# Second branch's scores: fp32 products over 64 rows, or two fp32r products over 128 rows

## The chip, the cores and the metric

The kernel runs on one core of one Trainium2 chip. The time is the device time of one execution in microseconds; the median of several runs is given. TensorE multiplies, VectorE (DVE), ScalarE (ACT) and GpSimd (POOL) do elementwise work, and SyncE (SP) issues nearly all transfers.

## The reference, cut to what matters

One layer of a decoder for 512 tokens of width 1024, all in float32. A token mixer with three attention branches is followed by a gated merge, an output projection and a SwiGLU. The change touches only the scores of the second branch, differential attention with 4 heads of 2 x 64 query and key columns:

```
logits = einsum('bqhmd,bshmd->bmhqs', q, k) * ATTN_SCALE + bias     # m = 0, 1; d = 64
p = softmax(where(dist >= 0, logits, -inf))
attn = p[:, 0] - lam * p[:, 1];   out = einsum('bhqs,bshe->bqhe', attn, v)
```

## The kernel before, in words

Large products are not made in plain fp32. Each operand is split into a rounded part (hi, type fp32r, a copy on ScalarE) and the rest (lo, a subtraction on VectorE), and TensorE adds three fp32r products, hi*hi, hi*lo and lo*hi (lines 862 to 864 and 1216 to 1218). The index scores of the first branch (lines 1025 and 1027) need two products: the query's hi part stands in 64 partitions and its lo part in the other 64, the key's hi part is doubled, and one product of 128 rows gives (hi+lo)*hi.

The attention is one loop over steps v = 0 to 87, written out in the same order on every engine (lines 1224, 1599, 2050). Steps 0 to 31 are the third branch, 32 to 63 the first (8 heads, 4 query blocks each), 64 to 79 the second (4 heads, 4 query blocks), and the rest are dense work. In the second branch a step is query block i = v % 4 of head h = (v - 64) // 4; it sees 128 * (i + 1) keys and has two score products, m = 0 and m = 1. Their operands lie in `bqk`, m = 0 in partitions 0 to 63 and m = 1 in 64 to 127; both are fp32 (line 1113), and each leaves two records in the trace.

In a step v from 66 on TensorE does, in order: the scores of v; 9 or 6 dense fp32r products of 512 columns for a tile `z` (none in steps 75 and 79); the transposes of the probabilities of v - 2; the products with the values of v - 3 (line 1160; line 1157 in the first branch). Scores go to two banks `s_ps`, one for each m, so a score product waits until VectorE has read the one two before it (`shifted`). Dense tiles have two banks `tile_ps`, freed by ScalarE (line 1442) or by VectorE's split (line 2038). VectorE, for step v: adds the bias to scores m = 0 (`shift`, line 2029), takes reciprocals, shifts m = 1, mixes the two probabilities of v - 1 (line 2069) after GpSimd has scaled one of them (line 798), makes the lo part of a weight chunk (line 1821, in steps 68 and 76 here), and splits tiles. ScalarE: exponentials (line 1580), copies of tiles, hi parts (1435), copies of transposed probabilities (1592).

Every engine works through its list in order. SyncE's list has 12 bias tables `tab` (line 642), each waiting for `shifted`, with four weight loads between them.

Of the kernel before, what the change touches and what calls it, by code (L numbers as in the profile page):

```python
# [66 lines left out]
OC_STEPS = (51, 57)  # L67
Z_STEPS = (66, 69, 72, 76, 80, 84)
# [155 lines left out]
def hybrid_block(nc, a, out):  # L224
# [10 lines left out]
    with ctx:  # L235
# [50 lines left out]
        ob_hi = place("ob_hi", R + 49, [P, 4, S], F32R)  # L286
        ob_lo = place("ob_lo", R + 57, [P, 4, S], F32R)
# [11 lines left out]
        w_uv = place("w_uv_sb", R + 121.25, [P, A_H, DH])  # L299

# [10 lines left out]
        e_raw = place("e_raw", R + 49, [P, 4, HW])  # L311
        e_lo = place("e_lo", R + 49, [P, 4, HW], F32R)
        e_hi = place("e_hi", R + 57, [P, 4, HW], F32R)
# [6 lines left out]
        mg_hi = place("mg_hi", R + 69, [P, KT, S], F32R)  # L320
# [105 lines left out]
        c_exp_made = sem("c_exp_made")  # L426
        lam_exped = sem("lam_exped")
# [30 lines left out]
        masked = sem("masked")  # L458
        recip_made = sem("recip_made")
# [13 lines left out]
        c_exped = sem("c_exped")  # L473
# [87 lines left out]
        def _(sp):  # L561
# [65 lines left out]
            load(20, [(KT, 0, cols(COL_Z, CW))])  # L627
            for n in range(A_H + B_H):
# [209 lines left out]
        def _(pe):  # L838
# [251 lines left out]
            def scores(k):  # L1090
# [20 lines left out]
                else:  # L1111
                    h, m = (v - MIX_B) // 4, k % 2
                    mm = pe.matmul(ps[:, 0:w], bqk[DH * m:DH * m + DH, h, i * P:(i + 1) * P],
                                   bqk[DH * m:DH * m + DH, 4 + h, 0:w], start=True, stop=True)
# [308 lines left out]
        def _(act):  # L1423
# [22 lines left out]
            act.activation(c_exp, c_col, ACT.Exp, scale=-1.0).then_inc(c_exp_made, 1)  # L1446
# [44 lines left out]
            act.activation(lam_e, lam_s, ACT.Exp).then_inc(lam_exped, 1)  # L1491
# [106 lines left out]

            for v in range(N_STEP):
# [22 lines left out]
                if v == 42:  # L1622
                    act.wait_ge(c_dif_made, 1)
                    act.activation(c_exp2, c_dif, ACT.Exp).then_inc(c_exped, 1)
# [180 lines left out]
        def _(dve):  # L1805
# [23 lines left out]
            dve.wait_ge(c_exp_made, 1)  # L1829
# [78 lines left out]
            dve.wait_ge(lam_exped, 1)  # L1908
# [139 lines left out]

            n_split = 0
# [369 lines left out]
```

## Time and profile before

| | us |
|---|---|
| median of 3 runs | 1000.14 |
| lowest and highest run | 998.85 and 1000.86 |
| span of the profiled execution | 997.8 |
| TensorE busy in the span | 982.7 (98%) |

The profiled execution is given by its span, from the first to the last instruction; the time around the span is not part of the page. The lowest and highest run are 1.05 and 3.06 us above that span. Busy time of TensorE is modelled: a matmul's record reaches beyond the start of the next one, so costs are best read from start to start.

### The profile page before, as it was taken

How to read it: one execution, taken by the hardware profiler on the slowest of the kernel's cores; microseconds unless marked ns; L12 is line 12 of the kernel's file. 1: busy time of each engine (PE TensorE's matmuls, PEld its weight loads, DVE VectorE, ACT ScalarE, POOL GpSimd, SP SyncE). 2: the span in 40 equal slices, each digit the busy share in tenths (PEclk: the TensorE clock that was granted, in tenths of full speed). 3: DMA queues.
4: the chain of work that ended last, by engine and by line, in shares of the span. 5: the costliest groups of instructions: out<-in, count | busy, mean ns of one | idle time of the engine just before them, and what ended most of it. 6: DMA issues, size and time to landing. Idle time of an engine off the chain costs nothing.

```text
span 997.8 us, 12705 instructions
## 1 busy us (share of the span) xinstructions
PE 982.7 (98%) x4925; PEld 804.8 (81%) x4925; DVE 481.4 (48%) x827; ACT 379.0 (38%) x679; POOL 103.2 (10%) x137
## 2 busy tenths in 40 slices
PE   7999999999999999999999999999999999999997
PEld 4778888878878767788888888988888888888886
DVE  3764778832245445664655563634433433331324
ACT  5355332254566657542223233533223222221322
POOL 1500000000065612100000002000000000000401
PEclk9999999999999999999999999999999999999999
DMA  8742836212131201265556642123444334232312
GB/s 329 230 126 85 282 119 184 90 43 85 64 108 33 64 23 33 74 207 169 191 170 211 232 139 84 64 84 105 119 150 146 111 105 148 84 106 85 127 43 85
DMA packets 88163, 123.13 MB, mean 123 GB/s; under 512 B 4824, under 2 KB 69941, under 8 KB 87986
## 3 DMA queue, kind: packets, MB, share of 16 engines
q1 hardware_dynamic: 87442, 115.98, 35.6%
q0 software_dynamic: 528, 6.22, 2.1%
q8 instruction: 32, 0.52, 0.2%
q10 hardware_dynamic: 144, 0.26, 0.1%
q14 instruction: 17, 0.14, 0.0%
HBM read 119.77 MB, written 8.45 MB: 128 GB/s over the span
## 4 chain that ended last, share of the span: by engine, by line
PE 94%; issue 2%; POOL 1%; DMA 1%; ACT 1%; DVE 0%; SPq 0%; POOLq 0%; DVEq 0%
PE tile_ps L862 18%; PE tile_ps L864 18%; PE tile_ps L863 18%; PE t_ps L1128 2%; PE o_ps L1157 2%; PE s_ps L1110 2%; PE tile_ps L1309 1%; PE s_ps L1309 1%; PE t_ps L1309 1%; PE tile_ps L1311 1%; PE s_ps L1311 1%; PE t_ps L1311 1%; PE tile_ps L1310 1%; PE s_ps L1310 1%; PE t_ps L1310 1%
## 5 line engine op out<-in xcount | busy, mean ns | idle before, releaser
L862 PE MATMUL tile_ps<-h_hi,w_hi 128*128 128x512 f32 x736 | 291.0, 395 | 0.2 <-ACT z L1442 0.2
L863 PE MATMUL tile_ps<-h_lo,w_hi 128*128 128x512 f32 x736 | 286.8, 390 | 0.0
L864 PE MATMUL tile_ps<-h_hi,w_lo 128*128 128x512 f32 x736 | 286.7, 390 | 0.0
L1821 DVE TENSOR_TENSOR w_lo<-w_raw,w_hi 128x2048 fp32r<-128x2048 f32 (+3 forms) x60 | 130.7, 2179 | 154.2 <-ACT w_hi L1435 153.5
L862 PEld LDWEIGHTS tile_ps<-h_hi,w_hi 128*128 128x128 f32 x736 | 138.1, 188 | 36.2 <-issue 6.6
L864 PEld LDWEIGHTS tile_ps<-h_hi,w_lo 128*128 128x128 f32 x736 | 138.1, 188 | 29.2
L863 PEld LDWEIGHTS tile_ps<-h_lo,w_hi 128*128 128x128 f32 x736 | 138.2, 188 | 27.6 <-issue 0.2
L1435 ACT ACTIVATE w_hi<-w_raw 128x2048 fp32r<-128x2048 f32 (+3 forms) x60 | 107.3, 1788 | 39.9 <-DMA w_raw<-in_w_branch_c_dram 9.2
L1818 DVE TENSOR_TENSOR t_lo<-t_raw,t_hi 128x2048 fp32r<-128x2048 f32 (+1 forms) x15 | 32.8, 2184 | 85.6 <-ACT t_hi L1433 85.5
L1433 ACT ACTIVATE t_hi<-t_raw 128x2048 fp32r<-128x2048 f32 (+1 forms) x15 | 27.0, 1799 | 81.5 <-PE s_ps L1311 53.5
L1580 ACT ACTIVATE nl<-nl,cst 128x256 f32<-128x256 f32 (+3 forms) x81 | 42.8, 530 | 33.0 <-DVE cst L2029 32.7
L1768 ACT ACTIVATE f_hi<-f_t 128x512 f32 (+1 forms) x22 | 13.9, 633 | 88.3 <-DVE f_t L2326 88.3
L784 POOL TENSOR_TENSOR tm<-tab,score 128x256 f32<-128x256 f32 (+2 forms) x24 | 26.6, 1107 | 177.2 <-DVE cst L2029 177.2
L1762 ACT ACTIVATE silu_t<-tile_ps 128x512 f32<-128x512 f32 x22 | 13.1, 599 | 72.0 <-PE tile_ps L864 71.9
L2326 DVE TENSOR_TENSOR f_t<-tile_ps,silu_t 128x512 f32<-128x512 f32 x20 | 13.8, 692 | 54.7 <-PE tile_ps L864 54.7
L1592 ACT ACTIVATE pt<-t_ps 128x128 f32<-128x128 f32 (+2 forms) x80 | 29.6, 408 | 21.4 <-PE t_ps L1128 20.3
L819 POOL TENSOR_TENSOR x<-gated,x 128x512 f32<-128x512 f32 x4 | 5.1, 1295 | 297.2 <-DVE gated L2247 297.2
L2165 DVE SCALAR_TENSOR_TENSOR ada_sum<-ada,cst,ada_sum 128x1024 f32<-128x1024 f32 x21 | 26.9, 1283 | 0.7
L1975 DVE MAX8 cst<-score 128x8 f32<-128x256 f32 (+2 forms) x48 | 25.1, 552 | 1.4
L1983 DVE MATCH_REPLACE8 score<-cst,score 128x256 f32<-128x256 f32 (+2 forms) x48 | 25.8, 543 | 0.0
L1128 PE MATMUL t_ps<-ident,nl 128*128 128x128 f32 x160 | 24.4, 274 | 0.0
L807 POOL TENSOR_TENSOR x<-gated,x_res 128x512 f32<-128x512 f32 x4 | 5.1, 1291 | 184.4 <-DVE gated L2247 184.4
(404 smaller groups left out, 1680.8 us busy)
## 6 DMA issues: line engine op xcount, KB each, us to landing
w_raw<-in_w_in_dram SPq DMA_DIRECT2D x31, 1024.0 KB, 5.6
w_raw<-in_w_gate_up_dram SPq DMA_DIRECT2D x22, 1024.0 KB, 6.9
ada<-in_w_ada_dram SPq DMA_DIRECT2D x12, 1024.0 KB, 5.5
t_raw<-in_w_down_dram SPq DMA_DIRECT2D x10, 1024.0 KB, 5.0
row_copies<-row_flat POOLq DMA_DIRECT2D x1, 5632.0 KB, 20.9
ada<-in_w_ada_dram SPq DMA_DIRECT2D x8, 640.0 KB, 12.0
ada<-in_w_ada_dram SPq DMA_DIRECT2D x8, 512.0 KB, 4.2
ada<-in_w_ada_dram SPq DMA_DIRECT2D x8, 384.0 KB, 9.6
```

The source lines that it names most:

```text
L862: pe.matmul(dst[0:mw, :], wh, x_hi[:, kx, :], start=start, stop=False)
L863: pe.matmul(dst[0:mw, :], wh, x_lo[:, kx, :], start=False, stop=False)
L864: mm = pe.matmul(dst[0:mw, :], wl, x_hi[:, kx, :], start=False, stop=stop)
L1128: mm = pe.transpose(t_ps[v % 2][:, j * P:(j + 1) * P], src[:, j * P:(j + 1) * P], ident[:])
L1309: pe.matmul(bank[:], x_hi[:, kx, blk], wh[:, kw, :], start=start, stop=False)
L1310: pe.matmul(bank[:], x_hi[:, kx, blk], wl[:, kw, :], start=False, stop=False)
L1311: mm = pe.matmul(bank[:], x_lo[:, kx, blk], wh[:, kw, :], start=False, stop=stop)
L1435: hi = nc.scalar.activation(w_hi[s][:, 0:kt, 0:n_cols], w_raw[s][:, 0:kt, 0:n_cols], ACT.Copy)
L1580: act.activation(b, b, ACT.Exp, bias=negmax[:, k:k + 1], scale=-1.0, accum_out=expsum[:, k:k + 1]).then_inc(exped, 1)
L1592: act.activation(pt[v % 2][:, 0:w], t_ps[v % 2][:, 0:w], ACT.Copy).then_inc(pt_ready, 1)
L1818: dve.tensor_tensor(t_lo[s][:, 0:wide, :], t_raw[s][:, 0:wide, :], t_hi[s][:, 0:wide, :].bitcast(F32), ALU.subtract).then_inc(w_split[s], 1)
L1821: dve.tensor_tensor(w_lo[s][:, 0:kt, 0:n_cols], w_raw[s][:, 0:kt, 0:n_cols], w_hi[s][:, 0:kt, 0:n_cols].bitcast(F32), ALU.subtract) \
```

## The change

The operands of the second branch's scores are stacked. For head h and m there are three new tiles of 128 x 512 in fp32r: `bq_st` (query hi in its own 64 partitions, query lo in the other 64), `bk_st` (key hi in both halves) and `bl_st` (key lo in its own half, zeros in the other). A score is then the sum of two fp32r products of 128 rows. Sixteen hi copies on ScalarE (one at the end of each of steps 42 to 45, 58 to 61, 66 to 69 and 70 to 73), sixteen subtractions on VectorE one step later, six of them behind a memset to zero, and eight transfers of 64 partitions x 2 KB within the SBUF, issued by SyncE behind the 5th, 9th, 11th and 12th bias table, prepare them. TensorE waits for them ahead of each head's first score. There are three sets of tiles; head 3 uses head 0's again. To make room, `ob_hi` and `ob_lo`, `e_raw`, `e_lo` and `e_hi` move to R + 69 and R + 77, and `mg_hi` moves to R + 49. Three one-off semaphores for small exponentials become one (`small_exped`), waited for at 1, 2 and 3; this is left out below.

```diff
 OC_STEPS = (51, 57)
+STACK_STEPS, TWICE_AFTER = (42, 58, 66, 70), (4, 8, 10, 11)
 Z_STEPS = (66, 69, 72, 76, 80, 84)
...
     return (v - 73) // 4 if 73 <= v <= 85 and (v - 73) % 4 == 0 else None
+def stack_hi_at(v):
+    for h, v0 in enumerate(STACK_STEPS):
+        if v0 <= v < v0 + 4:
+            return h, v - v0
+    return None
+def stack_of(h):
+    return h % 3
...
         oa_lo = place("oa_lo", R + 41, [P, 4, S], F32R)
-        ob_hi = place("ob_hi", R + 49, [P, 4, S], F32R)
-        ob_lo = place("ob_lo", R + 57, [P, 4, S], F32R)
+        ob_hi = place("ob_hi", R + 69, [P, 4, S], F32R)
+        ob_lo = place("ob_lo", R + 77, [P, 4, S], F32R)
         oc_hi = place("oc_hi", R + 93, [P, 2, S], F32R)
...
         w_uv = place("w_uv_sb", R + 121.25, [P, A_H, DH])
+        b_at = ((49, 51, 53, 55, 57, 59), (61, 63, 65, 67, 103, 105), (12, 14, 25, 107.25, 119.25, 121.25))
+        bq_st, bk_st, bl_st = ([[place(f"{n}{j}_{m}", R + b_at[j][2 * o + m], [P, S], F32R) for m in range(2)]
+                                for j in range(3)] for o, n in enumerate(("bq_st", "bk_st", "bl_st")))
...
             load(20, [(KT, 0, cols(COL_Z, CW))])
+            def key_twice(h):
+                j = stack_of(h)
+                for m in range(2):
+                    d0, d1 = DH * m, DH - DH * m
+                    sp.wait_ge(b_hi_made, 4 * h + m + 1)
+                    sp.dma_start(bk_st[j][m][d1:d1 + DH, :].bitcast(F32), bk_st[j][m][d0:d0 + DH, :].bitcast(F32)) \
+                        .then_inc(bk_twice[h % 2], 16)
             for n in range(A_H + B_H):
...
                 sp.dma_start(tab[n % 2][:], toeplitz(FL_AB + n * W_AB, W_AB, 1, S)).then_inc(tab_in[n % 2], 16)
+                if n in TWICE_AFTER:
+                    key_twice(TWICE_AFTER.index(n))
                 if n == 2:
...
                     h, m = (v - MIX_B) // 4, k % 2
-                    mm = pe.matmul(ps[:, 0:w], bqk[DH * m:DH * m + DH, h, i * P:(i + 1) * P],
-                                   bqk[DH * m:DH * m + DH, 4 + h, 0:w], start=True, stop=True)
+                    j = stack_of(h)
+                    if i == 0 and m == 0:
+                        pe.wait_ge(b_lo_made, 4 * h + 4)
+                        pe.wait_ge(bk_twice[h % 2], 32 * (h // 2) + 32)
+                    q_b = bq_st[j][m][:, i * P:(i + 1) * P]
+                    pe.matmul(ps[:, 0:w], q_b, bk_st[j][m][:, 0:w], start=True, stop=False)
+                    mm = pe.matmul(ps[:, 0:w], q_b, bl_st[j][m][:, 0:w], start=False, stop=True)
                 mm.then_inc(scores_made, 1)
...
+            def stack_hi(h, n):
+                j, m = stack_of(h), n % 2
+                if n == 0 and h < 2:
+                    act.wait_ge(o_made[1], MIX_A // 8)
+                elif n == 0 and h == 2:
+                    act.wait_ge(masked, 3 * A_H)
+                    wait_tile_made(act, ATT_TILE["qlat", A_H - 1])
+                elif n == 0:
+                    act.wait_ge(scores_made, MIX_B + 8)
+                rows = slice(DH * m, DH * m + DH)
+                act.activation((bq_st if n >= 2 else bk_st)[j][m][rows, :], bqk[rows, 4 - 4 * (n // 2) + h, :], ACT.Copy) \
+                    .then_inc(b_hi_made, 1)
             for v in range(N_STEP):
...
                         evacuate(ATT_TILE["qlat", h], qlat[h % 3][:, :])
+                if stack_hi_at(v) is not None:
+                    stack_hi(*stack_hi_at(v))
                 if ob_at(v) is not None:
...
                     dve.reciprocal(recip[:, u:u + 1], expsum[:, u:u + 1]).then_inc(recip_made, 1)
+            def stack_lo(h, n):
+                j, m = stack_of(h), n % 2
+                d0, d1 = DH * m, DH - DH * m
+                own, other = slice(d0, d0 + DH), slice(d1, d1 + DH)
+                dve.wait_ge(b_hi_made, 4 * h + n + 1)
+                if n >= 2:
+                    dve.tensor_tensor(bq_st[j][m][other, :], bqk[own, h, :], bq_st[j][m][own, :].bitcast(F32),
+                                      ALU.subtract).then_inc(b_lo_made, 1)
+                    return
+                if h < 3:
+                    if h == 1:
+                        wait_tile_made(dve, ATT_TILE["oc", 1])
+                    elif h == 2:
+                        wait_tile_made(dve, ATT_TILE["uv", A_H - 1])
+                    dve.memset(bl_st[j][m][other, :].bitcast(F32), 0.0)
+                dve.tensor_tensor(bl_st[j][m][own, :], bqk[own, 4 + h, :], bk_st[j][m][own, :].bitcast(F32),
+                                  ALU.subtract).then_inc(b_lo_made, 1)
...
                         .then_inc(oc_mixed, 1)
+                if v and stack_hi_at(v - 1) is not None:
+                    stack_lo(*stack_hi_at(v - 1))
                 h = (v - 71) // 4
```

## Rows read from the trace of the kernel before

**Rows 1.** The page, busy time: engine, microseconds, share of the span, instructions.
```profile
PE 982.7 (98%) x4925; PEld 804.8 (81%) x4925; DVE 481.4 (48%) x827; ACT 379.0 (38%) x679; POOL 103.2 (10%) x137
```

**Rows 2.** Windows: length, busy time of each engine, clock, share of DMA.
```profile
300.00:310.00 10.00, 10.00 (x64) 7.33 (x63) 5.58 (x20) 6.18 (x18) 5.17 (x7) 1.00 0.10 27
...
367.90:382.20 14.30, 14.13 (x79) 10.29 (x78) 8.64 (x26) 8.42 (x30) 2.44 (x4) 1.00 0.13 38
```

**Rows 3.** Timeline of TensorE, steps 71 to 73: start, length, engine, line.
```profile
379.09 1.13 PE L1113 MATMUL s_ps<-bqk 64*128 64x512 f32 x4
380.15 0.50 PE L862 MATMUL tile_ps<-h_hi,w_hi 128*128 128x512 f32 x1
380.49 0.40 PE L863 MATMUL tile_ps<-h_lo,w_hi 128*128 128x512 f32 x1
...
382.18 0.49 PE L1113 MATMUL s_ps<-bqk 64*128 64x128 f32 x4
382.60 0.50 PE L862 MATMUL tile_ps<-h_hi,w_hi 128*128 128x512 f32 x1
...
385.66 0.70 PE L1113 MATMUL s_ps<-bqk 64*128 64x256 f32 x4
386.29 0.50 PE L862 MATMUL tile_ps<-h_hi,w_hi 128*128 128x512 f32 x1
```

**Rows 4.** Line 1113's weight loads in step 69: ns min/median/max, first and last start.
```profile
L1113 PEld LDWEIGHTS s_ps<-bqk x4: 183/184/186, 370.7 to 370.8; 64*128 64x128 f32 x4
```

**Rows 5.** Chain of waits, three index score products of 256, 384, 512 columns.
```profile
75.78 0.12 PE s_ps L1025
...
77.41 0.17 PE s_ps L1025
...
79.15 0.23 PE t_ps L1025
```

**Rows 6.** Timelines of TensorE: eight loads of line 1160, one product of line 1177.
```profile
378.00 0.97 PEld L1160 LDWEIGHTS o_ps<-bv,pt 128*128 128x128 f32 x8
...
366.32 1.07 PE L1177 MATMUL tile_ps<-olat,w_uv_sb 128*64 128x512 f32 x2
```

**Rows 7.** Timelines of VectorE, then TensorE, round steps 68 to 70.
```profile
369.11 0.68 DVE L2038 TENSOR_TENSOR oa_lo<-tile_ps,oa_hi 64x512 fp32r<-64x512 f32 x1 [2.78 <-ACT oa_hi L1597]
369.83 0.29 DVE L2029 CUSTOM_DVE_ANT_0 nlb<-s_ps,tab 128x128 f32<-128x128 f32 x1
...
371.78 2.28 DVE L1821 TENSOR_TENSOR w_lo<-w_raw,w_hi 128x2048 fp32r<-128x2048 f32 x1
373.98 0.42 DVE L2029 CUSTOM_DVE_ANT_0 nl<-s_ps,tab 128x256 f32<-128x256 f32 x1
...
371.58 0.50 PE L862 MATMUL tile_ps<-h_hi,w_hi 128*128 128x512 f32 x1 [0.17 <-ACT z L1442]
...
374.96 0.92 PE L1113 MATMUL s_ps<-bqk 64*128 64x384 f32 x4
```

**Rows 8.** Timelines of TensorE, then VectorE, steps 75 and 76.
```profile
393.55 1.13 PE L1113 MATMUL s_ps<-bqk 64*128 64x512 f32 x4
...
396.13 0.49 PE L1113 MATMUL s_ps<-bqk 64*128 64x128 f32 x2 [0.19 <-DVE cst L2029]
...
394.71 0.69 DVE L2029 CUSTOM_DVE_ANT_0 nlb<-s_ps,tab 128x512 f32<-128x512 f32 x1 [1.28 <-PE s_ps L1113]
```

**Rows 9.** A group by line: shapes, count, busy us, mean ns, idle before.
```profile
L1679 ACT ACTIVATE mg_hi<-mg 128x512 fp32r<-128x512 f32 x8 | 4.9, 633 | 33.7 <-DVE mg L2191 33.7
```

**Rows 10.** Timelines of GpSimd, one form at two places, then VectorE beside the second.
```profile
277.11 0.37 POOL L793 TENSOR_SCALAR nl<-nl,cst 128x128 f32<-128x128 f32 x1
...
286.04 2.41 POOL L793 TENSOR_SCALAR nl<-nl,cst 128x128 f32<-128x128 f32 x1
...
285.74 2.47 DVE L1821 TENSOR_TENSOR w_lo<-w_raw,w_hi 128x2048 fp32r<-128x2048 f32 x1
```

**Rows 11.** DMA issues: count, size, median microseconds to landing.
```profile
tab<-row_copies SPq DMA_DIRECT2D x12, 256.0 KB, 2.7
```

More of the change, by code:

```diff
@@ L310, in hybrid_block @@
         t_lo = [place(f"t_lo{b}", 64 + 8 * b, [P, 4, HW], F32R) for b in range(2)]
-        e_raw = place("e_raw", R + 49, [P, 4, HW])
-        e_lo = place("e_lo", R + 49, [P, 4, HW], F32R)
-        e_hi = place("e_hi", R + 57, [P, 4, HW], F32R)
+        e_raw = place("e_raw", R + 69, [P, 4, HW])
+        e_lo = place("e_lo", R + 69, [P, 4, HW], F32R)
+        e_hi = place("e_hi", R + 77, [P, 4, HW], F32R)
         sig_a = place("sig_a", R + 17, [P, 2, S])
@@ L319, in hybrid_block @@
         ada2 = [place(f"ada2_{b}", R + 105 + 8 * b, [P, 2, D]) for b in range(2)]
-        mg_hi = place("mg_hi", R + 69, [P, KT, S], F32R)
+        mg_hi = place("mg_hi", R + 49, [P, KT, S], F32R)
         x_res = place("x_res", R + 33, [P, NBLK, D])
@@ L425, in hybrid_block @@
         kv_sq = sem("kv_sq")
-        c_exp_made = sem("c_exp_made")
-        lam_exped = sem("lam_exped")
+        small_exped = sem("small_exped")
         dn_used = sem("dn_used")
@@ L458, in hybrid_block @@
         masked = sem("masked")
+        b_hi_made = sem("b_hi_made")
+        b_lo_made = sem("b_lo_made")
+        bk_twice = [sem("bk_twice0"), sem("bk_twice1")]
         recip_made = sem("recip_made")
@@ L472, in hybrid_block @@
         c_dif_made = sem("c_dif_made")
-        c_exped = sem("c_exped")
         oc_mixed = sem("oc_mixed")
@@ L1445, in _ @@
             act.wait_ge(cols_ready, 1)
-            act.activation(c_exp, c_col, ACT.Exp, scale=-1.0).then_inc(c_exp_made, 1)
+            act.activation(c_exp, c_col, ACT.Exp, scale=-1.0).then_inc(small_exped, 1)
             for b in range(NBLK):
@@ L1490, in _ @@
             act.wait_ge(lam_dot, 1)
-            act.activation(lam_e, lam_s, ACT.Exp).then_inc(lam_exped, 1)
+            act.activation(lam_e, lam_s, ACT.Exp).then_inc(small_exped, 1)
             def query_hi(t):
@@ L1623, in _ @@
                     act.wait_ge(c_dif_made, 1)
-                    act.activation(c_exp2, c_dif, ACT.Exp).then_inc(c_exped, 1)
+                    act.activation(c_exp2, c_dif, ACT.Exp).then_inc(small_exped, 1)
                 if dense_ending_at(v) is not None and dense_ending_at(v)[0] == "z":
@@ L1828, in _ @@
             dve.tensor_copy(pcol, s_ps[0][:, 0:81]).then_inc(cols_ready, 1)
-            dve.wait_ge(c_exp_made, 1)
+            dve.wait_ge(small_exped, 1)
             link(dve.tensor_scalar(c_exp, c_exp, 1.0, None, ALU.add))
@@ L1907, in _ @@
             dve.tensor_scalar(g_sub_s, g_sub, 1.0 - LAM_INIT, None, ALU.mult)
-            dve.wait_ge(lam_exped, 1)
+            dve.wait_ge(small_exped, 2)
             link(dve.tensor_tensor(neg_lam, lam_e[:, 1:2], lam_e[:, 0:1], ALU.subtract))
@@ L2104, in _ @@
                 if v == 43:
-                    dve.wait_ge(c_exped, 1)
+                    dve.wait_ge(small_exped, 3)
                     dve.tensor_tensor(c_wgt[:, 0:16], c_exp2[:, 0:16], expsum[:, 0:16], ALU.mult)
```

## The prediction

> **What bounds the kernel now.** I read the page first: TensorE is busy for 982.7 of 997.8 us [rows 1], so time on its path counts, and time on another engine counts only where TensorE waits for it. Then the windows, to see which engine could run out in the stages that are touched: the granted clock is 1.00 throughout (the 2.4 GHz level), and VectorE is busy for 5.58 of 10 us in the first branch, where head 0's tiles would be made, but for 8.64 of 14.30 us in steps 68 to 71, beside ScalarE's 8.42 [rows 2]. There VectorE is the engine to watch. Then the timelines of TensorE and VectorE over steps 67 to 76, and the chain of waits over the index scores, which already have the form that the change brings in [rows 3 to 8].
>
> **TensorE, wide steps.** A step's two score products cost, from their start to that of the next instruction, 1.06 us for 512 columns (379.09 to 380.15), 0.85 for 384 (its group of 0.92 at 374.96, less the 0.07 by which the other groups reach past the next start), 0.63 for 256 (385.66 to 386.29) and 0.42 for 128 (382.18 to 382.60) [rows 3, 7]. The new form is four fp32r products, as the index scores have them: 0.23, 0.17 and 0.12 us each for 512, 384 and 256 columns [rows 5], hence 0.92, 0.68 and 0.48 us. That saves 0.14, 0.17 and 0.15 us; each width comes four times, so 0.46 x 4 = 1.84 us.
>
> Why so little, when half of the fp32 passes seem to go? Because the two old products do not follow one another. The four weight loads of a step start within 0.1 us, 370.7 to 370.8 [rows 4], and a single fp32 product of 128 rows and 512 columns is a group of 1.07 us [rows 6], nearly as long as both products of 64 rows together, 1.13 [rows 3]. So m = 0 and m = 1 run side by side in the two halves of the array, and stacking gives that up.
>
> The Trainium skill speaks against the change here (TensorE: Matmul & The Clock Gate, "Part 3: Packing small matmuls — row/col tiling"): products over few rows, placed in different row strips, run at the same time. By that rule the trace agrees, 1.06 us for two. Had they run one behind the other, a wide step would cost about 2.0 us and the change would save about 1.1 us in each.
>
> **TensorE, steps of 128 columns.** No fp32r product of 128 columns is in the trace. From below: eight weight loads of 128 columns take 0.97 us as a group, 0.19 the last [rows 6], so one starts every (0.97 - 0.19) / 7 = 0.11 us, and four products need 0.44 us against 0.42 now. From above: if such a short fp32r product were served like fp32, it would cost two of these slots, 0.22 us, and the step 0.88. I take 0.44, since 256 columns cost just 0.12 [rows 5] and half of that lies under the load's pace: four steps lose 0.08 us, and at the other end 1.84 us.
>
> **TensorE, change of type.** After fp32 work the first fp32r product delays its successor: 380.15 to 380.49 is 0.34 us where 0.23 is usual [rows 3, 5]. That 0.11 us now stands behind the scores, and will stand in front of them: no difference, except in steps 65, 75 and 79, which have no dense fp32r work and gain a change: 3 x 0.11 = 0.33 us lost. TensorE's own sum is 1.84 - 0.08 - 0.33 = 1.43 us saved.
>
> **Latency of the first score.** In a step of 512 columns VectorE starts on m = 0 at 394.71, 1.16 us after the scores began at 393.55 [rows 8]; the pair ends together. In the new order m = 0 takes 0.46 us, and with the 0.10 us between the pair's end and VectorE's start (1.16 - 1.06) and the 0.11 of the change of type it would be 0.67 us: VectorE starts 0.5 us earlier. This counts where a chain through VectorE holds TensorE. One place is step 76: its second score starts at 396.13 after a wait, because VectorE is still at step 75's scores [rows 8]. I book 0.5 us there, in place of step 75's own saving.
>
> **The preparation.** A hi copy of 64 x 512: the nearest row is a copy of 128 x 512 within the SBUF, 0.63 us on ScalarE [rows 9]; a subtraction of 64 x 512: 0.68 us on VectorE, at 369.11; records there overlap by 0.08 (371.78 + 2.28 against the next start at 373.98) [rows 7], so 0.6 us of the queue. A memset of 64 x 512 has no row: between nothing and the 0.68 of a subtraction. I take 0.4, since it reads nothing. So a subtraction behind a memset is 1.0 us. All in all VectorE gains 16 x 0.6 + 6 x 0.4 = 12 us of work, ScalarE 16 x 0.63 = 10. On ScalarE each copy ends a step's list, ahead of exponentials that wait for VectorE: I take it as hidden, bounds 0 and 0.6 us in step 68.
>
> For heads 0 and 1 I cost it at nothing: their work falls in steps 42 to 46 and 58 to 62 of the first branch, where VectorE is idle over 4 us in 10 [rows 2] and the scores run four steps ahead of their use. If that cover is thin, what is late is the reciprocal, with it GpSimd's scaling and the transposes; bounds 0 and 1 us. For head 3 too: steps 71 to 74, after the tight spot, bounds 0 and 0.6. The transfers land in about 2.7 us, as a table of 256 KB does [rows 11], and each is due steps later; on SyncE they wait for hi copies of an earlier step, so the weight load of chunk 23 queued behind them loses next to nothing, bounds 0 and 0.3. The moved tiles and the merged semaphore cost nothing: no order or wait changes with them.
>
> Head 2 is not free. Its first subtraction (with memset) stands in step 67 between VectorE's split at 369.11 and its shift at 369.83 [rows 7]. That shift is on TensorE's path: shift, exponentials, then ScalarE frees the bank of tile z, and the dense product at 371.58 has waited for exactly that [rows 7]. Against the 1.0 us stand the 0.5 us of latency in step 67, from which this chain starts, and the 0.19 us that TensorE had saved up to there (steps 64 to 66: -0.02 + 0.04 + 0.17): net the dense product is 0.31 us late. The second subtraction (again with memset) comes behind the weight chunk's lo part at 371.78 and ahead of the shift at 373.98: that shift is 0.31 + 1.0 late, done at 374.40 (its 0.42 us) + 1.31 = 375.71. The scores of step 70 (374.96 [rows 7]) need its bank: 0.75 us late, of which 0.17 comes back in that step. So TensorE enters step 71 0.58 us late, and all savings up to there are used up.
>
> **Sum.** Steps 71 to 79: 0.14 - 0.02 + 0.15 + 0.17 (steps 71 to 74), 0.5 (75 and the wait in 76), -0.02 (76), 0.15 + 0.17 + 0.03 (77 to 79) = 1.27 us. 1.27 - 0.58 = 0.69 us faster, so the span goes from 997.8 to about 997.1. The median stands 2.3 us above that span; what lies around it is unchanged, so 1000.14 - 0.69 = 999.4 us.
>
> **Rivals.** *All preparation is hidden.* For it: VectorE waits 1.28 us for TensorE before 394.71 and TensorE's wait at 371.58 is 0.17 us only [rows 7, 8]. Against it: the place of head 2's subtractions. The time: 1.43 + 0.5 - 0.03 (step 75's own share) = 1.9 us saved, 998.2.
>
> *The short steps lose.* One mechanism, in steps 64, 68, 72 and 76: fp32r of 128 columns at fp32's pace, 0.88 us in place of 0.42. That is 1.84 - 0.08 = 1.76 us on top: -0.69 + 1.76 = 1.1 us slower than before, 1001.2. It decides from 0.61 us a step on (0.69 / 4 + 0.44). For it only that no row shows such a product; against it the smooth 0.23, 0.17, 0.12 [rows 5].
>
> *VectorE's queue bites fully.* If the latency gain does not come, because the shifts are bound by VectorE's own work anyhow, steps 69 and 70 lose 0.5 us more and step 76 gives 0.5 less: -0.69 + 1.0 = 0.3 us slower, 1000.4. GpSimd could add to it: a scaling of 128 columns takes 0.37 us at one place and 2.41 at another, from 286.04 to 288.45, where VectorE was in a subtraction of two SBUF operands until 288.21 [rows 10]; the sixteen new ones are of that kind, and each could hold GpSimd for 0.6 us, with the mixing behind it. I put that at up to 1 us in steps 44 to 48, where a scaling comes right before its transposes: 1001.4 at worst.
>
> The Trainium skill has this as a rule (SBUF — State Buffer, the parts on the shared port pair): a VectorE instruction with two SBUF inputs and a GpSimd instruction that reads the SBUF exclude one another for the whole instruction. The trace agrees with it at 2.41 us.
>
> **Chances.** The forecast 0.48, with 998.8 to 1000.3 as its own range; all hidden 0.20; the short steps 0.14; VectorE's queue 0.18. What a measurement of this kernel can tell from no change is about 0.2%, 2 us. All hidden comes just short of it, and with luck in other waits passes it: faster by more than 0.2% 0.19. The short steps together with some of the queue would pass it upward: slower 0.13. Within 0.2%: 0.68. The range takes in the hidden case with its spread and the queue at its worst: 997.6 to 1001.8.
>
> **What would show it.** Four records of 0.23 us a wide step and groups of about 0.92 us show the saving; a first shift 0.67 us after the scores' start shows the latency. The price of 128 columns can be read in step 72 directly. A subtraction of 0.6 to 0.7 us and a memset right before the shifts of steps 68 and 69, and waits of TensorE for ScalarE's copy of z and for the shift ahead of step 70, show the loss; no such waits speak for the hidden case. Waits in steps 44 to 49 would show GpSimd held. The prediction is wrong in kind if the scores take more than 1.06 us at 512 columns, or if the stage from step 64 to 80 changes by more than 2 us either way.

## The result: slower by 0.33%, where no change was forecast

The changed kernel takes 1003.46 us (median of 7 runs, 1002.55 to 1004.03) where the kernel before takes 1000.67 us (7 runs). The ratio of the runs is 1.0033, with a 95% interval of 1.0023 to 1.0043 (the two medians alone give 1.0028). The forecast was 999.4 with a range up to 1001.8, so both time and range are missed. The profiled execution has a span of 1002.0 us against 997.8; these two lie further apart, by 4.2 us, than the ratio says (3.3), so the traces are read for where time goes, and the runs for how much it is in all.

The page's line of busy time, after, answers to [rows 1]:

```profile
PE 982.5 (98%) x4925; PEld 809.5 (81%) x4925; DVE 495.8 (49%) x849; ACT 386.7 (39%) x695; POOL 104.5 (10%) x137
```

TensorE is busy for as long as before, and the span is 4.2 us longer: TensorE waits more. VectorE has 14.4 us of new work and ScalarE 7.7. Two windows answer to those of [rows 2], the second again from the start of step 68 to that of step 72:

```profile
300.00:310.00 10.00, 9.65 (x60) 6.92 (x59) 6.50 (x21) 7.75 (x20) 3.64 (x6) 1.00 0.21 53
369.24:384.77 15.53, 13.65 (x79) 11.33 (x78) 12.40 (x32) 10.08 (x34) 2.45 (x4) 1.00 0.16 45
```

TensorE had 10.00 of 10 us in the first and now has 9.65. In the second VectorE is busy for 12.40 of 15.53 us (8.64 of 14.30 before), and TensorE, idle for 0.17 before, is idle for 1.88. The clock is 1.00 in both.

**Where the time went, step by step.** For each step I took the start of its scores in two traces and subtracted. The change of this difference from one row to the next is what the stage between them gained or lost; a constant part says nothing. (In e2 only head 0 is prepared, in e1 the products are the old ones; both are described below.)

```
start of the scores, us later than in the kernel before
step      after     e1       e2
42        +0.22   -0.86    +1.46
54, 62    +2.39   +1.30    +1.74     head 0's preparation lies between
68        +1.33   +1.30    +0.66
71        +2.95   +3.65    +0.04     head 2's
74        +2.02   +3.62    -0.89
77        +3.52   +4.98    -2.02     head 3's
79        +3.11   +4.99    -2.43
```

The changed kernel loses 2.17 us between steps 42 and 54, 0.72 net between 62 and 79, 0.8 right behind step 79 (the values' group of eight products, at 416.96 before, starts at 420.85, 3.89 late) and 0.3 in the 575 us behind that, which I did not follow. With the 0.22 at the start, which lies ahead of all of the change's work, this is the 4.2 us.

**The products themselves gain more than forecast.** Timeline of TensorE in the changed kernel, steps 71 and 72, which answers to [rows 3]:

```profile
382.04 0.48 PE L1146 MATMUL s_ps<-bk_st,bq_st 128*128 128x512 f32 x1
382.35 0.40 PE L1147 MATMUL s_ps<-bl_st,bq_st 128*128 128x512 f32 x1
382.58 0.39 PE L1146 MATMUL s_ps<-bk_st,bq_st 128*128 128x512 f32 x1
...
383.04 0.39 PE L890 MATMUL tile_ps<-h_hi,w_hi 128*128 128x512 f32 x1
...
384.77 0.31 PE L1146 MATMUL s_ps<-bk_st,bq_st 128*128 128x128 f32 x1
...
385.14 0.28 PE L1147 MATMUL s_ps<-bl_st,bq_st 128*128 128x128 f32 x1
385.25 0.45 PE L890 MATMUL tile_ps<-h_hi,w_hi 128*128 128x512 f32 x1
```

Read starts, not lengths: 382.04 to 383.04 is 1.00 us for 512 columns (before 1.06), 384.77 to 385.25 is 0.48 for 128 (before 0.42). An fp32r product of 128 columns starts every 0.11 to 0.12 us: the rival of the short steps is out. And yet e2's column falls by 0.36 us in a step of 512 columns (from 0.04 at step 71 to -0.32 at step 72), not by 0.06. The rest lies around the scores; section e4 has it.

**Head 2.** VectorE, then TensorE, in the changed kernel round steps 68 to 70, which answers to [rows 7]:

```profile
370.37 0.68 DVE L2087 TENSOR_TENSOR oa_lo<-tile_ps,oa_hi 64x512 fp32r<-64x512 f32 x1 [2.78 <-ACT oa_hi L1630]
371.11 0.48 DVE L2113 MEMSET bl_st<- 64x512 f32 x1
371.61 0.68 DVE L2114 TENSOR_TENSOR bl_st<-bqk,bk_st 64x512 fp32r<-64x512 f32 x1
372.22 0.28 DVE L2078 CUSTOM_DVE_ANT_0 nlb<-s_ps,tab 128x128 f32<-128x128 f32 x1
...
374.16 2.28 DVE L1870 TENSOR_TENSOR w_lo<-w_raw,w_hi 128x2048 fp32r<-128x2048 f32 x1
...
376.99 0.69 DVE L2114 TENSOR_TENSOR bl_st<-bqk,bk_st 64x512 fp32r<-64x512 f32 x1
377.71 0.42 DVE L2078 CUSTOM_DVE_ANT_0 nl<-s_ps,tab 128x256 f32<-128x256 f32 x1
```

```profile
372.56 0.39 PE L1146 MATMUL s_ps<-bk_st,bq_st 128*128 128x256 f32 x1 [0.46 <-DVE cst L2078]
...
373.95 0.50 PE L890 MATMUL tile_ps<-h_hi,w_hi 128*128 128x512 f32 x1 [0.62 <-ACT z L1475]
...
378.20 0.45 PE L1146 MATMUL s_ps<-bk_st,bq_st 128*128 128x384 f32 x1 [0.80 <-DVE cst L2078]
```

The chain is the one forecast: memset and subtraction before the shift (a second memset stands at 376.49), then the copy of z late (0.62, where e2, with nothing prepared for head 2, waits 0.26), then the scores of step 70 (0.80). It has one link more, the scores of step 69 (0.46).

**Head 3.** Three engines of the changed kernel, ahead of step 75 (ScalarE, VectorE, TensorE), which answer to [rows 8]:

```profile
393.99 0.63 ACT L1643 ACTIVATE bq_st<-bqk 64x512 fp32r<-64x512 f32 x1
394.65 0.69 ACT L1630 ACTIVATE ob_hi<-tile_ps,cst 128x512 fp32r<-128x512 f32 x1
```

```profile
388.37 0.69 DVE L2114 TENSOR_TENSOR bl_st<-bqk,bk_st 64x512 fp32r<-64x512 f32 x1
...
390.14 0.41 DVE L2078 CUSTOM_DVE_ANT_0 nl<-s_ps,tab 128x256 f32<-128x256 f32 x1
...
395.37 0.75 DVE L2089 SCALAR_TENSOR_TENSOR ob_lo<-tile_ps,cst,ob_hi 128x512 fp32r<-128x512 f32 x1 [3.08 <-ACT ob_hi L1630]
396.04 0.55 DVE L2078 CUSTOM_DVE_ANT_0 nl<-s_ps,tab 128x384 f32<-128x384 f32 x1
```

```profile
396.65 0.50 PE L1146 MATMUL s_ps<-bk_st,bq_st 128*128 128x512 f32 x1 [1.18 <-DVE cst L2078]
...
398.63 0.49 PE L1193 MATMUL o_ps<-bv,pt 128*128 128x128 f32 x2 [0.29 <-ACT pt L1625]
400.03 0.33 PE L1146 MATMUL s_ps<-bk_st,bq_st 128*128 128x128 f32 x1 [0.24 <-DVE cst L2078]
```

VectorE in e2, where head 3 is not prepared, at the same place:

```profile
385.79 0.41 DVE L2078 CUSTOM_DVE_ANT_0 nl<-s_ps,tab 128x256 f32<-128x256 f32 x1
...
390.23 0.75 DVE L2089 SCALAR_TENSOR_TENSOR ob_lo<-tile_ps,cst,ob_hi 128x512 fp32r<-128x512 f32 x1 [3.00 <-ACT ob_hi L1630]
```

TensorE waits 1.18 us at step 75 for VectorE's shift of step 74 (396.04). Ahead of this shift VectorE splits a tile of the output (`ob_lo`) and sits idle for 3.08 us until ScalarE has made the hi part. That idle time is not the preparation's: e2 has 3.00 us of it, and TensorE does not wait there. What grew is the delay of the whole chain. Against e2, TensorE's scores of step 73 start 2.91 us later (388.05 and 385.14), but VectorE's shift of step 73 starts 4.35 us later (390.14 and 385.79): 1.44 us are lost up to there. The subtraction at 388.37 stands ahead of it and holds the queue for 0.72 us; the mixing before that is 0.6 late already, because another subtraction (384.90) stands ahead of a small instruction (385.50) that GpSimd waits for before it scales. ScalarE's exponentials, its weight copy of 1.90 us and the hi part come behind this shift. Then the split is 5.14 us later (395.37 and 390.23), 0.79 more, with the copy at 393.99 right ahead of the hi part. So the chain arrives 2.23 us late, more than it had to spare. VectorE's subtractions cost the larger part, ScalarE's copy the smaller, and e11 below bears this out.

**Head 0.** VectorE, then GpSimd, in the changed kernel, steps 44 to 46:

```profile
303.10 0.48 DVE L2113 MEMSET bl_st<- 64x512 f32 x1 [1.37 <-ACT bk_st L1643]
...
310.18 1.67 DVE L2105 TENSOR_TENSOR bq_st<-bqk,bq_st 64x512 fp32r<-64x512 f32 x1
311.87 0.56 DVE L2078 CUSTOM_DVE_ANT_0 nl<-s_ps,tm 128x384 f32<-128x384 f32 x1
```

```profile
309.06 0.78 POOL L821 TENSOR_SCALAR nl<-nl,cst 128x128 f32<-128x128 f32 x1 [3.40 <-DVE cst L2096]
309.81 1.49 POOL L812 TENSOR_TENSOR tm<-tab,score 128x512 f32<-128x512 f32 x1
```

The shift at 311.87 started at 308.47 before. A subtraction of 0.69 us took 1.67, because GpSimd's mask was running from 309.81 to 311.30: the exclusion of [rows 10] with the roles changed. The Trainium skill (SBUF — State Buffer, the shared port pair) says that the loser is blocked until the other's instruction ends; 310.18 + 1.67 - 0.69 = 311.16 agrees within 0.15 us. TensorE then waits four times where it did not wait before (1.55 us in all): 0.35 us at 307.10 (for ScalarE's bv, behind a copy of head 0), 0.25 at 317.77 (for GpSimd's scaling), 0.34 and 0.61 at 326.17 and 328.53.

### The profile page after: what moved, and what is told of

It reads as the page before. It is cut to its first block, busy times and chain, and to the rows that moved or that the text cites. A ratio compares the mean times of both kernels' runs of the same rounds, so it can differ in the third digit from the quotient of the medians.

```text
span 1002.0 us, 12760 instructions
## 1 busy us (share of the span) xinstructions
PE 982.5 (98%) x4925; PEld 809.5 (81%) x4925; DVE 495.8 (49%) x849; ACT 386.7 (39%) x695; POOL 104.5 (10%) x137
## 4 chain that ended last, share of the span: by engine, by line
PE 88%; issue 4%; POOL 3%; ACT 2%; DVE 2%; DMA 1%; SPq 0%; POOLq 0%; DVEq 0%; ACTq 0%
PE tile_ps L890 17%; PE tile_ps L892 17%; PE tile_ps L891 17%; PE tile_ps L1344 1%; PE s_ps L1344 1%; PE t_ps L1344 1%; PE tile_ps L1343 1%; PE s_ps L1342 1%; PE t_ps L1342 1%; PE s_ps L1343 1%; PE t_ps L1343 1%; PE tile_ps L1342 1%; PE o_ps L1190 1%; PE t_ps L1161 1%; PE s_ps L1138 1%
```

## The experiments

**e1: the preparation alone.** The products are put back, all of the preparation stays:

```
-  pe.matmul(ps, q_b, bk_st[j][m], start=True, stop=False);  mm = pe.matmul(ps, q_b, bl_st[j][m], start=False, stop=True)
+  mm = pe.matmul(ps, bqk[DH*m:DH*m+DH, h, ...], bqk[DH*m:DH*m+DH, 4+h, 0:w], start=True, stop=True)
```

> The whole preparation of the changed kernel (16 hi copies, 16 subtractions, 6 memsets, 8 transfers, moved tiles, TensorE's waits for them), but the scores are made in the old form, two fp32 products of 64 rows. Theory queue (the loss is VectorE's and ScalarE's lists, into which the preparation was put ahead of shifts that TensorE waits for; the new products themselves save about 2 us): slower than the changed kernel by 1.5 to 2.5 us, about 1005.3, with TensorE late by about 2.2 us after step 54 and by about 2 more round step 70. Theory products (the new products cost more than the old ones, the preparation is hidden): as the kernel before, 1000.7.

Measured: 1005.14 us, ratio 1.0055 (1.0041 to 1.0068). The table gives the parts: 2.16 us up to step 54, 0 between 54 and 68 (head 1), 3.69 from 68 to 79. Nothing is lost behind step 79.

**e2: the new products alone.** Head 0 is prepared in steps 38 to 41, and its tiles serve all heads:

```
-                    j = stack_of(h)
+                    j = 0
```

> The new products, but only head 0's operands are prepared, in steps 38 to 41 in place of 42 to 45, and all four heads use them (so heads 1 to 3 are not computed from their own queries and keys). Theory queue: faster than the kernel before by 1.5 to 2.5 us, about 998.7, and TensorE gains about 1.4 us from step 64 on plus 0.5 at step 76. Theory products: slower than before or equal, 1000.7 to 1003. A step of 128 columns takes 0.44 us by the one and 0.88 by the rival on short products.

Measured: 997.25 us, ratio 0.9973 (0.9964 to 0.9982). The scores of steps 62 to 79 gain 4.17 us, of which 0.75 are lost again right behind step 79. The forecast had 1.9 for the products and the latency together.

The two parts do not add up. From step 62 to 79 e1 loses 3.69 us and e2 gains 4.17, which would be a gain of 0.48; the changed kernel loses 0.72. Up to step 71 they do add up (0.65 lost by the sum, 0.56 measured). The missing 1.2 to 1.3 us lie in steps 71 to 79: where TensorE waits for VectorE's chain at step 75, what its products have saved is not collected. So about half of head 3's price, as e5 and the table give it, is delay, and half is saving forgone.

**e3: head 0 earlier.** `STACK_STEPS = (38, 58, 66, 70)` in place of 42.

> The changed kernel with one number changed: head 0's operands are prepared in steps 38 to 41, ahead of the blending of the third branch's outputs on VectorE (steps 41 to 48), in place of 42 to 45. Theory queue: the 2.2 us that TensorE loses between steps 44 and 54 go, 1001.3. If the loss there is something else (the place of the tiles, the transfers), it stays: 1003.4.

Measured: 1002.07 us, ratio 1.0022 (1.0013 to 1.0031). In the trace head 0's price falls from 2.17 to 0.30 us: where it stood is what it cost. By the medians e3 is 1.4 us shorter than the changed kernel, by the ratios 1.1; with intervals of about 1 us to either side both agree with the 1.87 of the trace. The profiled execution gains 1.2 only, and its clock fell behind step 76. Windows of e3:

```profile
392.00:396.00 4.00, 2.81 (x16) 1.72 (x14) 2.74 (x8) 2.68 (x8) 0.56 (x1) 1.00 0.01 2
396.00:400.00 4.00, 3.74 (x11) 2.91 (x12) 2.89 (x13) 3.68 (x19) 2.08 (x3) 0.54 0.02 4
400.00:404.00 4.00, 4.00 (x18) 3.41 (x17) 3.59 (x5) 0.49 (x1) 0.38 (x1) 0.60 0.00 0
```

The sixth figure is the granted clock: TensorE runs for a good part of 8 us at 1.2 GHz, after its wait at step 75 (1.16 us). Between steps 76 and 77 the difference to the kernel before grows by 2.19 us. This holds for that execution, not for the median: such a fall shows as a mean granted clock of 0.995 over the execution, and only two of the eleven have it (1002.59 and 1002.70 us); the other nine, at 0.998 or 0.999, took 1000.63 to 1003.21.

**e4: no memset.** The zero halves go, and the second product takes its own 64 rows only:

```
-  dve.memset(bl_st[j][m][other, :], 0.0)
-  mm = pe.matmul(ps, q_b, bl_st[j][m][:, 0:w], start=False, stop=True)
+  mm = pe.matmul(ps, bq_st[j][m][own, ...], bl_st[j][m][own, 0:w], start=False, stop=True)
```

> The changed kernel without zero halves: the second product (query hi times key lo) takes only the 64 rows of its own half, and the six memsets (0.48 us each in the trace after) are gone. Theory queue: four of the six stand ahead of shifts that TensorE waits for, so 1.0 to 2.0 us faster than the changed kernel, about 1002. Theory products: no change from the memsets, and the second products of m = 0 and m = 1 cannot overlap, since a full product stands between them: 1003.4.

Measured: 1006.32 us, ratio 1.0068 (1.0054 to 1.0082). A miss, and the most telling one. Without its two memsets head 0 costs 1.15 us in place of 2.17; the loss is in the products. TensorE in e4, step 67:

```profile
365.87 0.48 PE L1146 MATMUL s_ps<-bk_st,bq_st 128*128 128x512 f32 x1
366.28 0.50 PE L1148 MATMUL s_ps<-bl_st,bq_st 64*128 64x512 f32 x1
366.71 0.50 PE L1146 MATMUL s_ps<-bk_st,bq_st 128*128 128x512 f32 x1
...
367.56 0.50 PE L890 MATMUL tile_ps<-h_hi,w_hi 128*128 128x512 f32 x1
367.90 0.39 PE L891 MATMUL tile_ps<-h_lo,w_hi 128*128 128x512 f32 x1
```

The same 512 columns that take 0.23 us between products of 128 rows take 0.43 where 128 and 64 rows alternate, and each weight load starts 0.24 us late:

```profile
366.71 0.19 PEld L1146 LDWEIGHTS s_ps<-bk_st,bq_st 128*128 128x128 f32 x1 [0.24 <-issue]
```

So a change of the row count costs about 0.2 us. The loads start late with nothing to wait for; from this I read, without a run that shows it apart, that a load for the other row count is not taken ahead of the running product. The kernel before paid this on both sides of its 64-row scores. Before: the values' eight products from 378.11 to the scores' start at 379.09 take 0.98 us, and the dense product behind, 380.15 to 380.49, 0.34. Here is the same place in e2:

```profile
378.32 1.05 PE L1193 MATMUL o_ps<-bv,pt 128*128 128x128 f32 x8
379.13 0.48 PE L1146 MATMUL s_ps<-bk_st,bq_st 128*128 128x512 f32 x1
...
380.13 0.39 PE L890 MATMUL tile_ps<-h_hi,w_hi 128*128 128x512 f32 x1
380.36 0.39 PE L891 MATMUL tile_ps<-h_lo,w_hi 128*128 128x512 f32 x1
```

0.81 in place of 0.98, 1.00 in place of 1.06, 0.23 in place of 0.34: 0.34 us a step, where the forecast saw 0.14. The Trainium skill (TensorE: Matmul & The Clock Gate, Part 3, "The mechanism") says in its list of what overlaps that loads overlap a running product only where their row strips differ; the paragraph above that list also allows a load into a background buffer. The traces agree for the two old 64-row halves, but loads of 128 rows behind 128 rows do overlap here (0.23 us a product), and only a changed row count does not.

**e5 and e6: without head 2, without head 3.** e3, with the head left out served by head 1's tiles:

```
+PREPARED = (0, 1, 3)        (e6: (0, 1, 2))
-                    j = stack_of(h)
+                    j = stack_of(h) if h in PREPARED else 1
```

> Head 0 prepared in steps 38 to 41 (as in e3_head0_early) and head 2 not prepared at all: its scores are taken from head 1's tiles, so the third head's output is not its own. Each head has its own price (theory): head 2's goes, 1.6 to 1.9 us, so 1000.2 +- 0.5, and the step table shows steps 68 to 74 as in e2_scores_only and head 3's 1.3 to 1.9 us in steps 75 and 76. Shared slack (rival): once head 2's delay is gone, head 3's waits go too, since they came from the backlog: 998 or less, as in e2_scores_only. Third: nothing but the clock's fall behind step 76 matters, then 1002, as e3.

> Head 0 in steps 38 to 41 and head 3 not prepared: its scores are taken from head 1's tiles, so the fourth head's output is not its own. Own price for each head (theory): head 3's waits at steps 75 and 76 go, 1.3 to 1.9 us, and where e3's executions had the clock's fall at 396 to 404 us (2.2 us) that goes with them: 1000.2 without the clock, 998.0 if the clock fell in every execution of e3; together with e5's gain it adds up to the 4.8 us between e3 (1002.07) and e2_scores_only (997.25). Rival (shared slack): about 998 here and in e5, the two gains adding up to far more than 4.8.

Measured: 999.04 us, ratio 0.9996 (0.9987 to 1.0004), and 998.67 us, 0.9989 (0.9980 to 0.9997). From step 62 to 79 e5 gains 1.53 us and e6 1.80, where e2 gains 4.17: head 3 costs 2.64 us and head 2 costs 2.37, in sum 5.0, against 4.89 in the changed kernel (0.72 + 4.17). Each head has its own price, and slack is not shared. The price of each is larger than the 1.6 to 1.9 I had read off as waits alone, which is part of why e5's time lies below its forecast of 1000.2. Neither trace shows the clock's fall (1.00 from 396 to 404 us), but three of e5's twelve executions have the mean clock of 0.995, and these take 1001.2 us on average where the other nine take 999.1.

**e7: less work on VectorE.** Keys of both m by one copy and one subtraction of 128 rows, the halves put in place by six transfers a head, the zero half replaced by the lo part again; head 0 in step 38:

```
+ act.activation(bk_st[j][0], bqk[:, 4 + h, :], ACT.Copy)                    (128 rows)
+ dve.tensor_tensor(bl_st[j][0], bqk[:, 4 + h, :], bk_st[j][0], ALU.subtract)
+ sp: for t in (bk_st[j], bl_st[j]): t[0][64:] -> t[1][:64] and t[1][64:];  once these landed, t[0][:64] -> t[0][64:]
```

> All heads prepared, from their own data, head 0 in step 38; but the keys of both m by one copy and one subtraction of 128 rows, and the halves put in place by six transfers a head; the second product's zero half becomes the lo part again (no memset). VectorE's work of a head falls from 3.7 us (head 3: 2.7) to 2.0, ScalarE's from 2.5 to 1.9. Theory (VectorE's queue): head 2 costs about 1 us in place of 1.9 and head 3 about 1 in place of 1.9: 1000.0 to 1000.5. Rival (waiting for ScalarE's copies, not VectorE's work, is what delays): 1001.5 to 1002, little better than e3. Second rival (transfers in two waves come late, 3 us each): TensorE waits on the transfers ahead of steps 72 or 76, 1003 and more.

Measured: 998.39 us, ratio 0.9983 (0.9975 to 0.9992). Better than expected: my figure had taken 1.9 us each for heads 2 and 3, which together had cost 4.89, and had kept e3's 0.30 for head 0. That is 1.1 us of the 1.9 by which it missed; the rest stays open. Heads 2 and 3 together now cost 2.32 us (4.17 less the 1.85 gained from step 62 to 79), head 0 nothing. The clock is 1.00 behind step 76, and no execution has the mean of 0.995.

**e8: head 2 earlier.** e7 with `STACK_STEPS = (38, 58, 62, 70)`.

> As e7_keys_whole, with head 2's three pieces in steps 62 to 65 in place of 66 to 69. Theory (place in VectorE's queue): head 2's price falls to 0 to 0.3 us, since steps 62 to 66 have idle time on VectorE, and head 3's 1 us stays: 999.2. Rival: the first branch's last steps, with their reciprocals and masks, are as tight as head 0's were in steps 44 to 54 (2 us): 1001 to 1002.

Measured: 998.55 us, ratio 0.9990 (0.9981 to 0.9999): no gain. Step 70 no longer waits and step 69 only for the 0.28 us that e2 has too, but TensorE in step 65 does, because a copy of head 2 at 355.38 stands ahead of ScalarE's evacuation of bv:

```profile
356.46 1.07 PE L1214 MATMUL tile_ps<-olat,w_uv_sb 128*64 128x512 f32 x2 [1.13 <-ACT bv L1479]
```

**e9: lo parts two steps after the hi copies.** `stack_lo(*stack_hi_at(v - 2))` in place of `v - 1`, in the changed kernel.

> The changed kernel, each lo part (with its memset) two steps after its hi copy in place of one; VectorE's work is the same. Theory A (VectorE's work delays): about as the changed kernel, 1003 to 1004, with head 0's 2.2 us now between steps 45 and 55. Theory B (VectorE's waits for ScalarE's copies delay; 1.37 us idle ahead of head 0's first memset): head 0's 2.2 us fall to about 0.8 and head 2's 1.9 to about 1.2: 1001.4.

Measured: 1005.54 us, ratio 1.0051 (1.0038 to 1.0065). Head 0 costs 2.3 us still (-0.29 at step 46, +2.04 at 54): not VectorE's wait for ScalarE ahead of the memset, theory B, but its work and what that meets. Nor does head 2 get cheaper: from step 62 to 74 it costs 2.35 us, 2.26 in the changed kernel. The loss beyond the forecast is at step 76, where head 3's last subtraction ends at 400.18 and TensorE, after 2.48 us, starts at 400.27, and the clock is at 0.50 in 400 to 404 us (mean 0.995 in four of the five executions).

**e10 and e11: other places.** Four sets of tiles in place of three (two of them in slices of bqk that head 1 has left), so that places can be chosen; (head, part, copy's step, subtraction's step):

```
+STACK_ORDER = ((0,0,38,39),(0,1,39,40),(0,2,40,41), (1,0,54,55),(1,1,55,56),(1,2,56,57),
+               (2,0,59,60),(2,1,60,61),(2,2,61,62), (3,0,66,67),(3,1,69,70),(3,2,72,73))
e11:                                                             (3,1,68,70),(3,2,69,72)
```

> As e7_keys_whole, with four sets of tiles: head 1 prepared in steps 54 to 57, head 2 in steps 59 to 62, head 3's keys in 66 and 67, its queries in 69, 70, 72 and 73, where the traces show both engines idle. Theory (place in the queues is all of the preparation's price): head 2's 1.2 us go, head 3's 1.15 us fall to 0.3 or less; with the products' saving of 4.2 us and 0.3 for step 79's change it comes to e2_scores_only's 997.25, at most 997.6. Rival: head 3 costs in the second branch wherever it stands: 998.2 or more, and the wait at step 75 stays.

> As e10_spread, with head 3's query copies in steps 68 and 69 (subtractions in 70 and 72), all ahead of the second weight chunk's copy of step 73. Theory (ScalarE's copies ahead of its 1.9 us weight copy are what makes step 75 wait in e7_keys_whole): as e10 or 0.3 us less. Rival (VectorE's subtractions): 0.3 us or more above e10, since step 70's queue is longer.

Measured: 998.26 us, ratio 0.9979 (0.9970 to 0.9988), and 998.56 us, 0.9985 (0.9976 to 0.9994). e10 misses its 997.6, though for another reason than its rival's: head 2 costs nothing and the wait at step 75 is gone, but 1.08 us are lost at step 56 (head 1, free in steps 58 to 61) and 0.4 at step 69. In e11 the scores of step 75 take 1.26 us again in place of 1.01, though all copies are over: against my theory, VectorE's subtraction in step 72 is enough for it. It stands ahead of the shift of step 73, which starts 1.06 us later than in e10 (387.14 and 386.08) where TensorE is 0.22 later. The two times alone don't tell e10 and e11 apart.

**e12: e3 once more, for the clock.**

> e3_head0_early once more, for its clock: if the granted clock falls to 0.5 to 0.6 behind step 76 whenever TensorE has waited there for 0.5 us or more, the windows of 396 to 404 us show it here too and the time is 1002.1; if it fell by chance in e3's profiled execution, they show 1.00 and the time of that execution is some 2 us shorter, 1000.4.

Measured: 1002.86 us, ratio 1.0026 (1.0015 to 1.0038). In the profiled execution the fall is there again, after a wait of 1.13 us at step 75:

```profile
396.00:400.00 4.00, 3.48 (x12) 2.60 (x13) 3.25 (x13) 4.00 (x19) 1.72 (x3) 0.62 0.02 6
400.00:404.00 4.00, 4.00 (x15) 3.31 (x14) 3.24 (x4) 0.52 (x2) 0.72 (x1) 0.52 0.00 0
```

But only three of the six executions have the mean clock of 0.995. So the same kernel falls in some executions and not in others (five of the seventeen of e3 and e12), and my "whenever" does not hold. Nor do the times follow it closely: the five average 1002.9 us, the other twelve 1002.2. The 2.2 us between steps 76 and 77 need thus not be what the fall costs a whole execution: in e5 the averages differ by 2.1, here by 0.7, and why stays open.

**e13: placed by the traces.** e10 with head 1 back in steps 58 to 61, head 2 in 61 to 64, and in step 67 the subtraction ahead of VectorE's split of tile uv:

```
-               (1,0,54,55),(1,1,55,56),(1,2,56,57), (2,0,59,60),(2,1,60,61),(2,2,61,62)
+               (1,0,58,59),(1,1,59,60),(1,2,60,61), (2,0,61,62),(2,1,62,63),(2,2,63,64)
+                if v >= MIX_B: (stack_lo here, ahead of split_lo(("uv", h)))
```

> As e10_spread, with head 1 back in steps 58 to 61, head 2 in 61 to 64 and, in the second branch, a subtraction ahead of VectorE's split of tile uv, for which VectorE waits for ScalarE (2.78 us idle in e10 at 366.6 to 369.4). Theory (the preparation costs only where it stands ahead of work that TensorE waits for): e10's 1.1 us at step 56 and 0.4 us at step 69 go, steps 46 to 79 change by 4.2 us as in e2_scores_only: ratio to before 0.9965, some 996.6. Rival (each piece costs something wherever it stands): as e10, 998, with waits in other steps.

Measured: 997.0 us (6 runs, 995.75 to 997.32) against 999.35 for the kernel before in the same runs, ratio 0.9971 (0.9959 to 0.9983). This version computes all heads and beats both kernels. VectorE in e10, then in e13, step 67:

```profile
369.35 0.69 DVE L2113 TENSOR_TENSOR oa_lo<-tile_ps,oa_hi 64x512 fp32r<-64x512 f32 x1 [2.78 <-ACT oa_hi L1649]
370.07 0.69 DVE L2129 TENSOR_TENSOR bl_st<-bqk,bk_st 128x512 fp32r<-128x512 f32 x1
```

```profile
365.87 0.68 DVE L2129 TENSOR_TENSOR bl_st<-bqk,bk_st 128x512 fp32r<-128x512 f32 x1
368.73 0.68 DVE L2113 TENSOR_TENSOR oa_lo<-tile_ps,oa_hi 64x512 fp32r<-64x512 f32 x1 [2.18 <-ACT oa_hi L1649]
```

The subtraction of bl_st now falls in the idle time ahead of the split and costs nothing. From step 62 to 79 e13 gains 3.83 us of e2's 4.17; the missing 0.34 is a wait for bv in step 65 (0.38 us at 357.16).

**e14: that one instruction alone.** e7, with the subtraction of step 67 ahead of the split.

> As e7_keys_whole, with one instruction moved: in step 67 head 2's first subtraction stands ahead of the split of tile uv in place of behind it. Theory: the 0.4 us that step 69 is long (1.40 for 0.98) go, step 70's delay stays (0.9), so 0.4 us less than e7: 998.0. Rival (ScalarE's copy, not VectorE's subtraction, delays the evacuation of tile z): nothing changes in step 69.

Measured: 997.94 us, ratio 0.9989 (0.9980 to 0.9998). The times don't tell it from e7. The trace does: step 69's scores take 0.98 us as in e2, in place of 1.40, and the gain from step 62 to 79 is 2.48 us in place of 1.85. So it was VectorE's subtraction, not ScalarE's copy, that held the chain through tile z; the part at step 70 stays (TensorE still waits 0.27 there).

## Why the prediction was wrong

A gain of 0.69 us was forecast; the traces show a loss of 4.2 (3.3 by the ratio of the runs). The difference of 4.9 us is 2.17 (head 0) + 1.43 (steps 71 to 79) + 1.05 (behind step 79) + 0.22 (the start, not the change's).

- *"For heads 0 and 1 I cost it at nothing", "bounds 0 and 1 us".* This step failed for head 0: 2.17 us, outside its bounds. Cover was judged by the mean of one window, VectorE busy for 5.58 of 10 us [rows 2]. The mean says nothing of order: the pieces stand ahead of reciprocals and shifts. What was "late next" was named rightly, the reciprocal and with it GpSimd. Moved by four steps the same work cost 0.30 us (e3). For head 1 the step held: 0 us.
- *"For head 3 too ... bounds 0 and 0.6".* Failed: about 2.6 us (e5). "After the tight spot" assumed that no chain was left there. There was one, through the shift of step 73, ScalarE's exponentials and weight copy, and the output's hi part to the shift of step 74: VectorE's subtractions were costed at nothing there, and delayed it by 1.44 us; ScalarE's copies were taken as hidden since each ends a step's list, and that ahead of the hi part added 0.8. TensorE waited 1.18 us for it. In steps 71 to 79 the products gained 2.47 us (e2, 0.04 to -2.43) and head 3 took 2.63: 0.16 lost where 1.27 gained was forecast.
- *Head 2.* The mechanism was right in each link (e14 shows the first alone), and TensorE enters step 71 0.56 us late (2.95 - 2.39) where 0.58 was forecast. But that is two wrong sizes which cancel: the head cost 2.26 us (2.95 - 2.39 against e2's 0.04 - 1.74), and the products had gained 1.70 by then. A link was missing, the scores of step 69. The pieces themselves were nearly right: the memset holds the queue for 0.50 us where 0.4 was assumed, the subtraction for 0.61 to 0.72 where 0.6 was.
- *"TensorE's own sum is ... 1.43 us saved".* Right in sign, wrong in size: 4.17 us with the latency (e2), where 1.43 + 0.5 was forecast. The durations of the scores were nearly right (0.92 forecast for 512 columns, 1.00 measured; 0.44 and 0.48 for 128). Missed was what they did to their neighbours: 0.17 us on the products ahead, 0.11 on the one behind. The 0.34 us of the dense product after the scores stood in [rows 3]; I put its 0.11 above the usual 0.23 down to the change of type, and so as paid on either side. In e2 0.08 us of it remain in front of the scores (the first product takes 0.31), and in e4 a change of the row count alone makes the same 0.34 (367.56 to 367.90). The latency itself came as forecast: in e10 the shift of step 75 starts 0.74 us after the scores (392.64 and 393.38), 0.67 forecast, 1.16 before.
- *The change of type in steps 65, 75 and 79.* Booked at 0.11 us each, it shows in step 65 alone (0.27 us from the last product's start to the next in place of 0.12, 358.49 to 358.76). Step 75 of e2 and step 79 of e3 take 1.01 us, like any other. What had no term in the sum is another loss, 0.75 to 0.8 us from step 79 on in e2, the changed kernel and e13 alike. TensorE's weight loads in the changed kernel wait there for VectorE's shifts of step 78 (0.16 and 0.24 us), for its mixing (0.42) and for ScalarE's copy of the probabilities:

```profile
411.87 0.20 PEld L1161 LDWEIGHTS t_ps<-ident,nl 128*128 128x128 f32 x2 [0.42 <-DVE nl L2137]
```

  The scores of step 79 take 1.26 us for it. In e3, where these scores start 1.42 us behind VectorE's first shift of step 78 in place of 0.61, and in e1 nothing is lost there. So this too is saving that TensorE could not collect, because VectorE's chain was next.
- *Rivals.* "VectorE's queue bites fully" named the mechanism and put it at 1001.4 at worst; the preparation's whole price came to 7.1 us (2.17 + 4.89), saving forgone included (5.85 in e1, without the new products); GpSimd's part in it was real, in the other direction. "The short steps lose" is refuted (0.48 us), "all hidden" too.

## What to carry to other kernels

Do not cost added work by an engine's busy share in a window. For each piece write down what is queued directly behind it on its engine and which engine waits for that, over the whole chain: here two subtractions of 0.7 us on VectorE and a copy of 0.6 us that ended a step's list on ScalarE put one shift off by 2.2 us. An engine's idle time in such a chain is no room to spare if it waits for another link. A piece put into an idle stretch a few instructions earlier costs nothing (e13). And where TensorE waits for the chain, a saving on TensorE is not collected. When a product changes its number of rows, look at the starts of its neighbours as well as at its own.

## What was not expected of the hardware

- A change between products of 64 and of 128 rows costs TensorE some 0.2 us: 0.41 to 0.43 us for each product of 512 columns in e4, against 0.23 between equals. On the neighbours of the old 64-row scores it was 0.17 and 0.11 us.
- GpSimd holds VectorE just as VectorE holds GpSimd: a subtraction of 0.69 us took 1.67 beside a mask of 1.49 us.
- The granted clock fell to 0.5 to 0.6 behind step 76 in the profiled executions of e3, e12 and e9, with 2.2 us lost between two steps in e3, but stayed at 1.00 in the changed kernel, whose wait at step 75 was as long (1.18 us against 1.16 in e3). By the mean clock it comes and goes from one execution of a kernel to the next: two of eleven in e3, three of six in e12, three of twelve in e5, four of five in e9, none of seven in the changed kernel. What tips it stays open.
- Six transfers of 64 x 512 a head, in two waves, never made TensorE wait in e7, e8, e10 or e13.
